# Rotary angle arithmetic and its two sines moved to the first stage, and one transpose of keys moved ahead of a query projection

## The reference

```python
for i in range(DEPTH):                                   # DEPTH = 2
    x = x + 0.5 * swiglu(rmsnorm(x, ln_ff1[i]), w_ff1_in[i], w_ff1_out[i])
    h = rmsnorm(x, ln_mix[i])
    x = x + (short_conv_mixer(h, ...) if i == 0 else sliding_window_attention(h, positions, ...))
    x = x + 0.5 * swiglu(rmsnorm(x, ln_ff2[i]), w_ff2_in[i], w_ff2_out[i])
return rmsnorm(x, ln_final)

def rope_tables(positions, dtype):                       # the angles and their cosines and sines
    inv_freq = ROPE_THETA ** (-jnp.arange(0, HEAD_DIM, 2, dtype=jnp.float32) / HEAD_DIM)
    ang = positions.astype(jnp.float32)[..., None] * inv_freq
    return jnp.cos(ang)[:, :, None, :].astype(dtype), jnp.sin(ang)[:, :, None, :].astype(dtype)
```

## Time and profile before

| | |
|---|---|
| median of 3 runs | 935.27 us (935.02 to 935.29) |
| the profiled execution, own time | 935.29 us |
| its span in the profile | 933.5 us |
| PE busy | 918.5 us, 98% of the span |
| DVE busy | 732.1 us, 78% |
| ACT busy | 440.6 us, 47% |
| POOL busy | 27.2 us, 3% |
| DMA | 168.83 MB, 180 GB/s read over the span |

### The profile page before, as it was taken

One profiled execution on the slowest core, in us unless ns is written; L12 is line 12 of the kernel. 1 busy time (PEld: TensorE's weight loads), 2 busy tenths in 40 slices (PEclk: granted clock), 3 DMA queues, 4 the chain that ended last, 5 costly groups with the idle time before them and its releaser, 6 DMA issues.

```text
span 933.5 us, 12971 instructions
## 1 busy us (share of the span) xinstructions
PE 918.5 (98%) x4203; PEld 758.1 (81%) x4203; DVE 732.1 (78%) x1286; ACT 440.6 (47%) x615; POOL 27.2 (3%) x55
## 2 busy tenths in 40 slices
PE   7999999999999999999999999999999999999996
PEld 6788888788888888888888888888878888888885
DVE  5988888768756988888889888887676689888884
ACT  6453444456444444435365353444575463444432
POOL 1000000000000000000000000000411000000000
PEclk9999999999999999999999999999999999999999
DMA  8765665448624665656457565664350187565622
GB/s 267 231 214 191 188 217 179 153 144 291 225 96 157 209 216 179 204 179 197 149 172 246 178 196 191 188 216 136 136 180 5 47 283 230 184 219 178 200 94 70
DMA packets 122101, 168.83 MB, mean 181 GB/s; under 512 B 8588, under 2 KB 98772, under 8 KB 122068
## 3 DMA queue, kind: packets, MB, share of 16 engines
q1 hardware_dynamic: 121936, 168.35, 56.2%
q10 hardware_dynamic: 132, 0.04, 0.0%
HBM read 167.31 MB, written 1.05 MB: 180 GB/s over the span
## 4 chain that ended last, share of the span: by engine, by line
PE 87%; DVE 5%; DMA 3%; ACT 2%; issue 2%; POOL 0%; SPq 0%; DVEq 0%; POOLq 0%; ACTq 0%
PE acc L1115 28%; PE proj L1099 18%; PE proj L1101 18%; PE proj L1100 18%; DVE scratch L783 2%; DVE in_lo L711 2%; DMA raw_out<-in_w_ff_out 1%; DVE out_lo L718 1%; PE tp L1150 1%; ACT in_hi L424 1%; DMA raw_in<-in_w_ff_in 1%; PE tp L1163 1%; DMA raw_in<-in_attn_w_qkv 1%; PE proj L1291 1%; PE acc L1317 1%
## 5 line engine op out<-in xcount | busy, mean ns | idle before, releaser
L1099 PE MATMUL proj<-in_hi,xT_hi 128*128 128x512 f32 x848 | 332.2, 392 | 0.9 <-DVE gated L774 0.6
L1101 PE MATMUL proj<-in_hi,xT_lo 128*128 128x512 f32 x848 | 330.1, 389 | 0.0
L1100 PE MATMUL proj<-in_lo,xT_hi 128*128 128x512 f32 x848 | 330.0, 389 | 0.0
L711 DVE TENSOR_TENSOR in_lo<-raw_in,in_hi 128x1024 fp32r<-128x1024 f32 x212 | 251.1, 1224 | 41.5 <-ACT in_hi L424 41.0
L424 ACT ACTIVATE in_hi<-raw_in 128x1024 fp32r<-128x1024 f32 x212 | 212.8, 1050 | 16.9 <-PE proj L1101 6.0
L468 ACT ACTIVATE gated<-proj,rstd 128x256 f32<-128x256 f32 x88 | 41.7, 474 | 337.1 <-PE proj L1101 337.0
L783 DVE STREAM_TRANSPOSE scratch<-gated 32x128 f32<-32x128 f32 x640 | 193.5, 302 | 8.3
L1099 PEld LDWEIGHTS proj<-in_hi,xT_hi 128*128 128x128 f32 x848 | 159.2, 188 | 36.0 <-issue 1.3
L1101 PEld LDWEIGHTS proj<-in_hi,xT_lo 128*128 128x128 f32 x848 | 159.2, 188 | 33.1
L1100 PEld LDWEIGHTS proj<-in_lo,xT_hi 128*128 128x128 f32 x848 | 159.3, 188 | 32.4
L718 DVE TENSOR_TENSOR out_lo<-raw_out,out_hi 128x1024 fp32r<-128x1024 f32 x96 | 113.7, 1222 | 13.2 <-ACT out_hi L432 11.9
(11 more groups left out here) (105 smaller groups left out, 442.5 us busy)
## 6 DMA issues: line engine op xcount, KB each, us to landing
raw_in<-in_w_ff_in SPq DMA_DIRECT2D x352, 256.0 KB
raw_out<-in_w_ff_out SPq DMA_DIRECT2D x88, 512.0 KB, 4.2
raw_in<-in_conv_w_in SPq DMA_DIRECT2D x24, 512.0 KB
raw_in<-in_attn_w_qkv SPq DMA_DIRECT2D x12, 512.0 KB
raw_out<-in_conv_w_out SPq DMA_DIRECT2D x8, 512.0 KB, 5.5
raw_out<-in_attn_w_o SPq DMA_DIRECT2D x8, 512.0 KB, 3.7
x<-in_x SPq DMA_DIRECT2D x2, 512.0 KB, 4.8
scratch<-in_ln_final SPq DMA_DIRECT2D x1, 512.0 KB, 4.3
```

The costliest lines, as they stand in the source:

```text
L711: dve.tensor_tensor(in_lo[:, slot, 2 * q:2 * q + 2, :], raw_in[:, 2 * q:2 * q + 2, :], in_hi[:, slot, 2 * q:2 * q + 2, :].bitcast(F32), AL ...
L1099: pe.matmul(proj[t][:, :], x_hi, in_hi[:, slot, k, :], start=(k == 0), stop=False)
L1100: pe.matmul(proj[t][:, :], x_hi, in_lo[:, slot, k, :], start=False, stop=False)
L1101: last = pe.matmul(proj[t][:, :], x_lo, in_hi[:, slot, k, :], start=False, stop=(k == KD - 1))
```

## The change

Three edits. DVE runs `rope_angles` in stage 0, after `split_out` of unit 0 and before `middle(1, 1)`, in place of stage 2. ACT waits for `trig_arg` and runs its two sines in stage 0, also after `split_out` of unit 0 and before `middle(1, 1)`, in place of stage 3. PE transposes the keys of token tile 1 (`transpose_qk(1)`) before the projection `queries(1, 1)`, in place of after it.

```diff
@@ ACT
-                    if s == 3:
+                    if s == 0:
                         act.wait_ge(trig_arg, 1)
                         act.activation(sin_t[:, :, :], angle[:, :, :], ACT.Sin).then_inc(trig_ready, 1)
                         act.activation(cos_t[:, :, :], turns[:, :, :], ACT.Sin).then_inc(trig_ready, 1)
@@ DVE
                     move_hidden(c)
                     split_out(o, o % 2)
+                    if s == 0:
+                        rope_angles()
...
                             middle(LOOP_FROM + 2 * i + b, b)
-                    if s == 2:
-                        rope_angles()
                     j = NJ - 1
@@ PE
                     queries(1, 0)
                     transpose_qk(0)
+                    transpose_qk(1)
                     queries(1, 1)
-                    transpose_qk(1)
                     transpose_qk(2)
```

## The result

The changed kernel takes 943.15 us in the median of 5 runs (942.18 to 944.5), against 935.27 (935.02 to 935.36): ratio 1.0092, 95% interval 1.008 to 1.0103. It is 0.8 to 1.0% slower; 939.7 was forecast, 938.6 to 942.0 as the range. Nine more runs of the changed kernel on record lie between 942.87 and 945.74. The profiled execution has 943.97 us of its own, span 942.1, against 935.29 and 933.5: 8.68 us more.

A forecast was written before the change was run, and what follows sets the result against it. PE was taken to bound the kernel, busy 918.5 of 933.5 us. The sum was 935.29 + 3.91 (edits 1 and 2) + 0.54 (edit 3) + 0 = 939.7 us, range 938.6 to 942.0.

The forecast's parts named there:

- Edit 1, the angles: Stage 0, DVE: the angles ahead of L774 and L790 delay PE's first products by their full 2.91 us.
- Edit 2, ACT's part of 1.00: Stage 0: ACT's SiLU and `hidden_hi` queue behind the sines' wait for the angles, adding 1.00 us to PE's delay.
- Stage 2 gives nothing back: End of stage 2: removing the angles gains between 0 and 0.16 us, taken as 0.
- Given back or growing: After stage 0's first products: the 3.91 us delay is neither recovered nor grows; 0 to 0.3 us, taken as 0.
- Edit 3, the wait of 2.48: Stage 4: PE stands from 669.35 to 671.83 before `transpose_qk(1)`, for POOL's last sum; 2.48 us lost.
- Edit 3, the three waits go: Stage 4: later waits of 0.95, 0.48 and 0.51 us vanish, 1.94 back; net 0.54 us slower.
- The clock: Granted clock of PE: the forecast sum included no loss from it; a fall was left to a rival.
- the first rival: Stage 0: the clock falls in the 4.4 us wait, costing 1.95 us more, 941.6 us; chance 0.18.
- The signs of being wrong: Stage 0 PE wait under 3 us, end of stage 2 nearer by over 1 us, or stage 4 shorter.
- expected sights: Profile signs: starts 3.9 us later up to stage 4, PE standing 2.2 to 2.5 there, no clock below 1.00 after 38.8.

The follow-up runs named there:

- edit 1 alone: Kernel before with the angles moved to stage 0 and the two sines left in stage 3: 940.14 us, ratio 1.0053.
- edit 3 alone: Kernel before with only `transpose_qk(1)` moved ahead of `queries(1, 1)`: 936.70 us, ratio 1.0017.
- the repetition: The changed kernel itself, unaltered, timed once more beside the kernel before: 942.88 us, ratio 1.0077.
- edits 1 and 2 alone: Kernel before with the angles and the two sines moved to stage 0, key transpose left in place: 940.72 us, ratio 1.0057.

## Why the prediction was wrong

Direction right, size too small by 3.4 us: 7.9 in place of 4.4.

- **Edit 1, the angles:** the step that put all 2.91 us on PE held. They start where forecast and take 2.93 to the end of L817 (33.14 to 36.07), and moving the place alone took the cost to zero.
- **Edit 2, ACT's part of 1.00:** held. The wait of 3.43 with edit 1 alone and 4.39 with both are 0.96 apart. First products at 38.16 where 38.77 less the 0.59 that PE came earlier is 38.18.
- **Stage 2 gives nothing back:** held; the wait at its end is 0.23 after and was 0.16 before.
- **Given back or growing:** "I put 0 to 0.3 on that" held. No wait was seen after the products, and none in the three profiles with spare work either, where the products ran at the full pace.
- **Edit 3, the wait of 2.48:** mis-sized. It measured 3.43. I took the end of POOL's last sum from one execution, asked only whether it could come earlier, and did not ask whether it could come later. What does set it is DVE's L711 beside it: in the run before, the last weight piece landed late (ACT stood 2.44 us for it), DVE had a gap, and the fourth sum ran alone in 0.45. In later profiles it took 1.43 and 1.53 (changed kernel), 1.43 (edit 3 alone) or 0.45 (the three kernels with spare work). Over the profiles of the kernels that leave POOL's order as it was, it took 0.45 or 0.46 where ACT stood 1.55 us or more for that piece and 1.43 or more where it stood 1.45 or less. The term is 2.5 or 3.4, by when the transfer lands.
- **Edit 3, the three waits go:** held, 1.94 us back. With 3.43 less 1.94 the net is 1.5, not 0.54; edit 3 alone at full clock measured 1.57.
- **The clock:** this is the step that failed: the sum put it at nothing. I gave a fall, as the first rival, 0.18, one place and 1.95 us. It came at both places: 2.16 us in the 24 products of stage 0, and in stage 4 about 1.5 (six slow matmuls and a slow transpose: `queries(1, 1)` from 678.63 to 685.37 is 6.74, where 5.58 was usual, and the transpose ahead of it 0.77 where 0.41 was). Together 3.7, and in the repetition 1.3 and 2.7. Spare work in both waits took both falls away; that its time is 3.7 lower as well is in part chance, as 0.9 of it is POOL's. The error was to read a threshold out of the earlier trace rows: 4.8 us of quiet before the one fall I could see. In stage 0 the clock fell 2.4 us after PE had gone quiet (33.6 to 36.0) in the changed kernel, 4.0 in its repetition and 2.1 with edits 1 and 2 alone; in stage 4 after 3.3 and 2.5, and with 17 spare matmuls in stage 0 even when PE was at work again; with edit 3 alone it did not fall in a wait of 3.5. One fall bounds nothing from below. I had also priced the wait of stage 4 without it. The price of 1.95 was not read from a stretch at the low level either: over the earlier trace rows the windows from 4 to 10 us give a granted clock of 1.00, though the transposes there take about twice the 0.107 us of the spare ones.
- **The signs of being wrong:** none of the three fired. Three of the expected sights did fail: the starts at the head of stage 4 were 5.1 later (674.08 against 669.00) and not 3.9, PE's wait there was 3.19 idle and not 2.2 to 2.5, and the clock was below 1.00 behind 38.8.

What stays open: edits 1 and 2 alone cost 5.4 and edit 3 alone 1.4, in sum 6.8, while both together cost 7.5 to 7.9. The falls of the clock differ from run to run, and one or two profiles for each kernel do not settle whether that is all. What decides whether the clock falls in a given wait is open too.

## What to carry to other kernels

- Small work is free or costly by its place. Ask of the engine whether the result queued behind it is the one that the bound engine waits for: 2.9 us of DVE work cost nothing where PE had slack, and 4.8 ahead of L790, the clock included. A wait put on a second engine (ACT) made two engines that ran side by side run one after the other.
- A new wait of TensorE, of the lengths seen here (2.5 to 4.4 us), is to be priced with a stretch at half clock behind it, here 1.3 to 2.7 us, and with a spread; a lone fall in a trace gives no safe length. Split the neighbouring work and put the waiting instruction where its input is ready.
- A start taken from one profile is only as fixed as what runs beside it on a shared path: ask what else could shift, transfers included.

## What the runs showed of the hardware

- The granted clock fell in or just behind waits of 2.5 to 4.4 us and stayed at half for about 6.8 us in some places (36.0 to 42.8 in stage 0 of the changed kernel, 676.1 to 682.9 in stage 4 of its repetition) and 3.4 in others (677.7 to 681.1, 37.8 to 41.2), so part of the low stretch can lie in the wait itself. A wait of 3.5 us (edit 3 alone) and one of 2.46 (transposes as spare work, stage 4) passed with the clock at 1.00.
- 17 matmuls of 512 columns or 44 transposes of 128 in a wait kept the clock at 1.00.
- POOL's additions of 128x128 took 0.45 us alone and 1.4 beside DVE's two-input subtractions, those of 128x256 0.73 and 1.6 to 1.8. With the angles at the end of stage 0, POOL's fourth sum began at 670.63, 0.15 us before DVE's L711, and took 0.46, while that L711 took 1.39 in place of 1.23; in the repetition L711 began at 675.55, 0.01 before the sum, and the sum took 1.53.
